# Two hybrid mixers of a float32 transformer kernel: VectorE's work beside the input products in another order

## What is computed

```python
h = rmsnorm_2(x, norm1[layer]); proj = h @ w_in[layer]      # 1024 -> 12 tiles of columns
# six heads of 64: gated delta rule, in chunks of 64 tokens
qkv = silu(causal_conv(concat(q, k, v), conv_w))            # four taps along the sequence
q, k = l2norm(q) * 64**-0.5, l2norm(k)
a_mat = where(strict, (k*beta) @ k.T * decay, 0)            # 64 x 64 per chunk and head
u, w = solve(a_mat + eye, [v*beta, k*beta*exp(G)])          # unit lower triangular
qk = where(causal, q @ k.T * decay, 0);  q_dec = q * exp(G)
# then the scan over chunks with the state; six heads of forgetting attention; pooling; @ w_out
```

## Time and profile before

| | us |
|---|---|
| median of 3 runs | 1598.57 |
| lowest, highest | 1598.29, 1599.12 |
| the profiled execution, its own time | 1598.96 |
| its span, first to last instruction | 1597.1 |

### The profile page before, as it was taken

The page is one execution under the profiler, slowest core; times in us unless marked ns, Lnnn a source line. Parts: engine busy times, 40 slices in busy tenths (PEclk is TensorE's granted clock), DMA queues, the critical chain, the costliest instruction groups (busy, mean ns, idle before and its releaser), DMA issues.

```text
span 1597.1 us, 26689 instructions
## 1 busy us (share of the span) xinstructions
PE 1548.6 (97%) x9862; PEld 1317.0 (82%) x9862; DVE 1214.9 (76%) x1499; ACT 1018.5 (64%) x1413; POOL 25.0 (2%) x37
## 2 busy tenths in 40 slices
PE   7999999999999999999999999999999999999998
PEld 6987888878878888888778888988788888888886
DVE  6677877765678777787775556887688988898887
ACT  5666656565576666765564545854577777777775
POOL 0000000000000000110000000200000000000000
PEclk9999999999999999999999999999999999999999
DMA  7534554535425455462255553631469999999994
GB/s 265 188 136 169 194 198 175 193 134 185 156 100 208 178 199 184 144 204 85 97 192 186 184 208 135 192 134 55 184 263 364 351 347 356 358 363 349 354 368 157
DMA packets 48521, 339.01 MB, mean 212 GB/s; under 512 B 5824, under 2 KB 6000, under 8 KB 8496
## 3 DMA queue, kind: packets, MB, share of 16 engines
q1 hardware_dynamic: 46368, 330.94, 56.5%
q0 software_dynamic: 2064, 6.83, 1.6%
HBM read 336.66 MB, written 1.10 MB: 211 GB/s over the span
## 4 chain that ended last, share of the span: by engine, by line
PE 48%; DVE 5%; ACT 5%; issue 1%; DMA 0%; DVEq 0%; ACTq 0%; SPq 0%
PE PS L1688 16%; PE PS L1706 8%; PE PS L1793 5%; PE PS L844 5%; PE PS L1813 4%; PE PS L1794 3%; ACT MWH L2017 1%; DVE MWL L2826 1%; DVE ARENA L3257 1%; PE PS L1647 1%; PE PS L1737 1%; PE PS L1671 1%; DVE ARENA L3157 0%; PE PS L1348 0%; PE PS L1610 0%
## 5 line engine op out<-in xcount | busy, mean ns | idle before, releaser
L3473 DVE TENSOR_TENSOR EWL<-W,EWH 128x2048 fp32r<-128x2048 f32 x144 | 329.2, 2291 | 45.0 <-ACT EWH L2546 44.8
L1793 PE MATMUL PS<-HTB,WH 128*128 128x512 f32 x992 | 347.4, 394 | 1.6 <-DVE HTB L2799 1.6
L2546 ACT ACTIVATE EWH<-W 128x2048 fp32r<-128x2048 f32 x144 | 276.3, 1919 | 65.8 <-PE PS L1706 36.8
L1794 PE MATMUL PS<-HTB,WL 128*128 128x256 f32 x1056 | 295.8, 280 | 0.0
L844 PE MATMUL PS<-MWH,HTB 128*128 128x512 f32 (+1 forms) x960 | 250.3, 345 | 4.7 <-DVE MWL L2826 2.3
L2821 DVE TENSOR_TENSOR WL<-W,WH 128x2048 fp32r<-128x2048 f32 x99 | 226.5, 2288 | 36.6 <-ACT WH L1999 33.5
L1999 ACT ACTIVATE WH<-W 128x2048 fp32r<-128x2048 f32 x99 | 189.6, 1919 | 98.1 <-PE PS L1794 88.8
L2826 DVE TENSOR_TENSOR MWL<-W,MWH 128x1024 fp32r<-128x1024 f32 x138 | 168.0, 1223 | 99.8 <-ACT MWH L2017 97.7
L1793 PEld LDWEIGHTS PS<-HTB,WH 128*128 128x128 f32 x992 | 186.2, 188 | 46.3 <-issue 2.2
L2017 ACT ACTIVATE MWH<-W 128x1024 fp32r<-128x1024 f32 x138 | 144.6, 1055 | 122.6 <-PE PS L844 121.7
L1794 PEld LDWEIGHTS PS<-HTB,WL 128*128 128x128 f32 x1056 | 198.7, 188 | 1.0
(11 more groups left out here) (381 smaller groups left out, 2354.8 us busy)
## 6 DMA issues: line engine op xcount, KB each, us to landing
W<-in_weights SPq DMA_DIRECT2D x312, 1024.0 KB, 5.0
ARENA<-rows_m POOLq DMA_DIRECT2D x8, 192.0 KB, 7.5
ARENA<-rows_m POOLq DMA_DIRECT2D x2, 768.0 KB, 9.4
CS<-in_consts POOLq DMA_DIRECT2D x3, 403.0 KB, 4.5
X<-in_x SPq DMA_DIRECT2D x2, 512.0 KB, 3.9
out<-X SPq DMA_DIRECT2D x4, 256.0 KB, 2.8
PR<-in_params SPq DMA_DIRECT2D x1, 830.0 KB, 10.2
CS<-in_consts POOLq DMA_DIRECT2D x2, 403.5 KB, 4.7
```

Source lines behind the costliest of these rows:

```text
L1793: mm(PS[b][:, :], WH[:, sl, o:o + P], HTB[:, :, kk, :], start=(kk == 0), stop=False, skip_group_check=True)
L1794: ins = mm(PS[b][:, 0:256], WL[:, sl, o:o + P], HTH[:, kk, :], start=False, stop=(kk == KC - 1), skip_group_check=True)
L2546: A(EWH[tile % SPLIT][:, :], tile_ap(w0 + tile), ACT.Copy).then_inc(sem("moe_hi"), 1)
L3473: TT(EWL[tile % SPLIT][:, :], tile_ap(w0 + tile), EWH[tile % SPLIT][:, :].bitcast(F32), SUB).then_inc(sem("moe_lo"), 1)
```

## The change

One ScalarE call and the calls of VectorE's mixer2 change places; no instruction is added or taken away. convolved gets an argument for a part of its taps, so that convolved(3) can be issued in two pieces (tap 1, then taps 2 and 3), with its marks kept in conv_last between them. convolved(2) moves from behind decayed() to ahead of normed(1); normed(1), normed(2) and KB now come before fd(11), and KB before the small product; convolved(3) is split around masked(1) and fd(14); fd(16) becomes fd(15) behind update(1) and fd(17) behind masked(2); masked(2) to masked(5), the updates, the values, QD, normed(3), normed(4) and the weight splits are interleaved anew as the diff shows. On ScalarE, last_inverse() moves ahead of fd(25).

```diff
--- before.py
+++ after.py
@@ -2480,8 +2480,8 @@
             next_tile(10)
             key = (m, "in", 10)
             release(A(m2.FV[:, :, P:384], v3(bank(key)[:, :], 2), ACT.Copy), key)
+            last_inverse()
             fd(25)
-            last_inverse()
             for t in range(NT):
                 key = (m, "u", t)
                 await_full(act, key)
@@ -3243,20 +3243,23 @@
                     ins = dve.tensor_reduce(st_mx[:, 2 * h + n:2 * h + n + 1], m2.SM[:, h % 2, sl], AX.X, MAX, negate=True)
                 ins.then_inc(sem(m + "f_mx"), 1)
 
-            def convolved(j):
+            conv_last = {}
+
+            def convolved(j, steps=(1, 2, 3)):
 
                 key = (m, "in", j)
                 dve.wait_ge(sem(m + "_c0"), j + 1)
                 us = [u for u in (2 * j, 2 * j + 1) if u < 9]
-                last = {}
-                for s in (1, 2, 3):
+                for s in steps:
                     for u in us:
                         if s > 1:
-                            after(last[u])
+                            after(conv_last[u])
                         o = (u % 2) * 256
                         ins = STT(m2.Y[:, u, s:256], bank(key)[:, o:o + 256 - s], taps[:, u, 3 - s:4 - s], m2.Y[:, u, s:256], MUL, ADD)
                         if s < 3 or u != us[-1]:
-                            last[u] = mark(ins)
+                            conv_last[u] = mark(ins)
+                if s < 3:
+                    return
                 ins.then_inc(sem(m + "_c1"), 1)
                 if j < 4:
                     dve.wait_ge(sem(m + "_c1"), j + 1)
@@ -3264,10 +3267,11 @@
 
             def betas():
 
+                dve.wait_ge(sem(m + "_kb_in"), 32)
+                TT(m2.KB, m2.QKN[:, 0:3, :], m2.KB, MUL).then_inc(sem(m + "_kb"), 1)
+                fd(11)
                 await_free_of(dve, (m, "rowT"))
                 link(TT(st_beg, st_tm[:, :, 2, :], st_tm[:, :, 0, :], MUL))
-                dve.wait_ge(sem(m + "_kb_in"), 32)
-                TT(m2.KB, m2.QKN[:, 0:3, :], m2.KB, MUL).then_inc(sem(m + "_kb"), 1)
 
             def score_masks():
 
@@ -3320,37 +3324,39 @@
             fd(8)
             convolved(1)
             fd(10)
+            convolved(2)
             normed(1)
-            fd(11)
             normed(2)
             betas()
             fd(12)
             decayed()
-            convolved(2)
             fd(13)
+            convolved(3, (1,))
             masked(1)
             fd(14)
-            convolved(3)
-            fd(16)
+            convolved(3, (2, 3))
             update(1)
+            fd(15)
             masked(2)
+            fd(17)
+            update(2)
             fd(18)
             convolved(4)
-            update(2)
             masked(3)
             keys_turned()
+            fd(19)
+            update(3)
+            fd(20)
+            masked(4)
             normed(3)
-            fd(20)
-            update(3)
+            values_turned()
+            fd(21)
+            update(4)
+            normed(4)
+            fd(22)
+            masked(5)
             dve.wait_ge(sem(m + "_egb"), 1)
             TT(m2.QD, m2.QKN[:, 3:6, :], m2.EGB, MUL).then_inc(sem(m + "_qd"), 1)
-            masked(4)
-            values_turned()
-            fd(22)
-            normed(4)
-            update(4)
-            masked(5)
-            fd(23)
             normed(5)
             normed(6)
             fd(24)
```

## The result

The changed kernel takes 1589.47 us (median of 4 runs, 1586.64 to 1591.42), the kernel before 1598.84 beside it (median of 4): a ratio of 0.9938, 95% interval 0.9921 to 0.9956. That is 9.4 us faster, with 7.0 to 12.6 by the interval; 10.6 was forecast, 1588.0 with a range of 1586.2 to 1591.5. The profiled execution happens to be the fastest of the four, 1586.64 (span 1584.8).

What follows compares the result with a forecast made beforehand. TensorE bounds the mixers, so only its idle time can be won: 11.3 us of waits plus 1.0 of overlap, less 1.0 (scores_0), 0.5 (kT) and 0.2 (lo 11), gives 10.6, so 1588.0 us, range 1586.2 to 1591.5.

Steps and rivals of the forecast that it cites:

- Seven waits a mixer: TensorE's waits in the second block's two mixers: 14 waits, 11.3 us, plus 0.07 of lost overlap each, 12.3 at most.
- scores_0's new wait: Mixer's end: scores_0 would wait 0.5 us for banks that the two multiplications by the decay free.
- kT's: kT's second half would wait about 0.25 us a mixer for masked(3)'s bank, since convolved(4) stands ahead of masked(3).
- the 0.2 at half 11 in m1: Front of m1: lo 11, behind KB, ends at 1028.9 where TensorE wants it at 1028.7; 0.2 us given back.
- convolved(2) beside GpSimd at no cost: Ahead of normed(1), convolved(2) fills VectorE's 2.45 us hole; with one input in PSUM, GpSimd's sum adds nothing.
- The slack ahead of half 13: Without convolved(2) ahead of it, lo 13 ends 0.7 us before TensorE wants it; the 1.15 us wait is saved.
- update(1) in time: update(1) starts at 705.2, its banks free at 706.3, M(2) wants them at 708.1; 1.28 us wait saved.
- The last copy: ScalarE's copy of the inverse's half ahead of fd(25): corrected_values' 0.78 us wait saved, 0.85 with the overlap.
- The waits of the later M steps: For s = 2 to 4 VectorE is ready when D(s) ends, so the next M never waits; 0.96 and 0.34 us saved.
- rival 1: Front of mixer: GpSimd holds convolved(2), or KB's data lands later; 1589 to 1591 us, 1591.2 if fully held; chance 0.20.
- My own sign of being wrong: The prediction is wrong if VectorE still releases more than 1.5 us of TensorE's waits in a mixer.
- Rival 3: Late KB landing holds VectorE, then TensorE; slower beyond 5.8 us late, for instance 1601.8 us; chance 0.05 with other losses.

Runs made afterwards that it cites:

- two_sbuf: Changed kernel with convolved(2) reading a constant in SBUF instead of its tile in PSUM; mixer stretches 93.13 and 92.28 us against 89.75.
- conv2_back: Changed kernel with convolved(2) put back behind decayed(); mixer stretches 91.56 us in m0 and 92.51 in m1 against 89.75.
- fd16_ahead: Changed kernel with fd(16) ahead of update(1) instead of fd(15) behind it; mixer stretches 90.56 us in m0 and 91.81 in m1 against 89.75.
- copy_back: Changed kernel with ScalarE's last_inverse() behind fd(25) again; mixer stretches 91.51 and 91.18 us against 89.75, 89.9 in both without waits the edit can't cause.
- copy_only: Kernel before the change with only ScalarE's last_inverse() moved ahead of fd(25); mixer stretches 94.53 us in m0 and 94.95 in m1, against 95.14 and 95.02.
- after_again: The changed kernel measured and profiled once more, unedited; median 1589.7 us, ratio 0.994 to the kernel before, mixer stretches 89.72 and 91.15 us.
- guard: Changed kernel in which GpSimd's first sum (L824) also waits until lo 10 is done; median 1589.28 us, ratio 0.994 to the kernel before.
- kb_late: Changed kernel with GpSimd's two DMAs for KB issued behind the two for the attention's bias; 1598.79 us, mixer stretches 94.33 and 95.81.

## Why the prediction was right

**Term by term.** Seven waits a mixer, 11.3 us and 1.0 of overlap, were all taken away. scores_0's new wait came out at 0.61, not 0.5; kT's at 0.29, for 0.25; the 0.2 at half 11 in m1 did not show in this profile, since KB's data landed by 1021.7, with m1 itself 4.6 us earlier. Sum of the mixers: 10.7 for 10.6. That it meets to 0.1 is partly luck: with these two waits, and 0.07 of overlap at scores_0, the terms add up to 10.4, and no row here says where the other 0.3 comes from.

**convolved(2) beside GpSimd at no cost** held, and is shown by two_sbuf rather than only argued. **The slack ahead of half 13** and **update(1) in time** are shown by conv2_back and fd16_ahead within 0.2 us. **The last copy** is shown by copy_back and copy_only: in the changed kernel most of its gain goes to the next waiter. The waits of the later M steps (0.96 and 0.34) and of vT (0.28) are gone from the profile too, but no run puts their part of the order back by itself, so which move removed each is argued, not shown.

**Where it was off.** The medians gain 9.4 and 9.2, not 10.6. Both intervals hold 10.6 as well (7.0 to 12.6 and 7.5 to 11.5 us), so the medians alone don't show a shortfall. But 1589.47 lies outside my sum's band, 1587.2 to 1589.0, and inside that of rival 1, 1589 to 1591, whose second half (KB's data lands later) came true in part and whose first (convolved(2) is held) did not; the stated range was met with rival 1's share in it. My own sign of being wrong, VectorE as the releaser of more than 1.5 us of waits in a mixer, is absent from the changed kernel's first profile and there in the second one's m1: 1.1 at kk, 0.2 at half 11 and 0.6 at scores_0. So the term that was mis-sized is the front of the mixer, which I took at its best: KB "just in time", with 0 lost in m0 and 0.2 in m1. Of the changed kernel's two profiles one lost nothing, the other 1.4 us in m1. Two things make that loss, and both were made dearer by the change: KB's DMA lands later than VectorE wants it (0.25 to 1.5 us of waiting in most profiles, kb_late's apart), and lo 10 is held by GpSimd's L824. I had priced GpSimd against the moved instruction (rival 1), not against the one ahead of it, whose delay convolved(2) now hands on to KB. Before the change a held lo 10 cost 0.5 us (copy_only's m1), after it 1.4 (after_again's m1); these are single mixers, and guard, which prevents it, did not bring the median down by an amount that shows.

**Rival 3** (slower, by KB's landing) was priced too mildly. kb_late lost the whole gain with VectorE held 3.5 and 4.6 us for KB; I had put the turn at 5.8 us behind the latest landing. The step of this rival that failed is "a microsecond of landing behind 691.8 moves all of TensorE's work by one": with waits of 2.77 and 3.99 us at kk the clock fell as well.

**What stays open.** Why lo 10 is held although L824's record starts behind the point where lo 10 would have ended, by 0.1 to 0.3 us in six of the seven cases: guard's two mixers in that range show that ordering the two prevents it, not what is taken early. And the spread between executions, 3.4 to 5.8 us in the versions with five or more, is only partly explained: the clock behind m1 (0, 3.4 or 6.8 us at the low level; over all fourteen profiles TensorE's way from half 23 of m1 to the start of its last matmul took 500.5, 501.2 to 501.3, and 502.9 to 503.1 us with them) and KB's landing are two shares of it.

## What to carry to other kernels

Filling an engine's hole with later work can be free in the profile one reads, but whatever delays the filler's predecessor now reaches everything behind the filler: price the instruction ahead of the hole as well. When several waits on one engine are removed, follow each shared buffer to its next taker; 0.85 us gained at corrected_values left 0.2, and moving masked(3) ahead gave 0.29 and cost 0.57. A gain of less than 0.7% on a kernel that spreads by 0.3% is better measured as a stretch of the timeline than as a total.

## What the runs showed of the hardware that was not expected

- A VectorE instruction with two inputs in SBUF (lo 10) was held in each of the seven mixers in which, without guard, the record of a GpSimd sum (L824) starts 1.07 to 1.53 us behind its own: 4.0 to 4.5 us instead of 1.23, ending 1.1 behind the sum. GpSimd's next sum then takes 2.28 instead of 1.48.
- TensorE's wait of 2.77 us was followed by 3.4 us at 1.2 GHz, from 1.6 us behind it on, and cost 1.5 us more; one of 3.99 went with 6.8 us of it, from 1.9 us into the wait on, and cost 2.0 more. A wait of 1.57 in two_sbuf's m0 was followed by 3.4 us of it too, one of 2.20 in its m1 by none.
- KB's two DMAs of 192 KB landed 3.3 to 9.0 us after their issue over all profiles but kb_late's (8.0 to 9.9 there). In the changed kernel VectorE comes for them 7.3 us behind the second issue (692.13 - 684.8 in m0), which is less than the longest of these landings.
